# Each expert slab as two half-row transfers in place of one

## The reference

```python
def expert_choice_ffn(h, w_router, w_gate, w_up, w_down):
    cap = EC_CAPACITY * S // N_EXPERTS                 # 64 tokens for each of 16 experts
    aff = softmax(einsum('bsd,de->bse', h, w_router))
    gates, idx = lax.top_k(aff.transpose(0, 2, 1), cap)
    xe = h[bidx, idx]
    a = jnp.einsum('becd,edf->becf', xe, w_gate)       # [64 x 1024] @ [1024 x 2048], per expert
    b = jnp.einsum('becd,edf->becf', xe, w_up)         # the same shape
    ye = jnp.einsum('becf,efd->becd', jax.nn.silu(a) * b, w_down)   # [64 x 2048] @ [2048 x 1024]
    return jnp.zeros_like(h).at[bidx, idx].add(ye * gates[..., None])
```

## Time and profile before

| what | value |
|---|---|
| median of 3 runs | 2109.13 us |
| the runs | 2108.97 to 2114.0 us |
| the profiled execution | 2113.66 us |
| its span, from the first to the last instruction | 2111.9 us |
| PE busy in it | 1956.1 us, 93% |
| DMA over the whole span | 528.11 MB, mean 250 GB/s |
| mean granted clock of TensorE | 0.978 of full speed |

### The profile page before, as it was taken

The page is one execution under the profiler, slowest core; times in us unless marked ns, Lnnn a source line. Parts: engine busy times, 40 slices in busy tenths (PEclk is TensorE's granted clock), DMA queues, the critical chain, the costliest instruction groups (busy, mean ns, idle before and its releaser), DMA issues.

```text
span 2111.9 us, 23315 instructions
## 1 busy us (share of the span) xinstructions
PE 1956.1 (93%) x9049; PEld 1144.9 (54%) x9049; DVE 845.5 (40%) x1273; ACT 592.5 (28%) x917; POOL 36.7 (2%) x40
## 2 busy tenths in 40 slices
PE   7888889999999999999999988999999999999898
PEld 5656633322222222222222266888888778778786
DVE  6765431111111111111111165456456576876443
ACT  5553321110011000110010044443233343356651
POOL 1004000000000000000000000000000000000000
PEclk9988999999999999999999988999999999999999
DMA  8421579999999999999999952545345222221101
GB/s 256 140 90 35 202 292 422 422 422 422 422 422 422 422 422 422 422 422 422 422 422 422 422 183 100 198 132 186 130 160 181 80 80 81 90 70 40 41 21 40
DMA packets 132179, 528.11 MB, mean 250 GB/s; under 512 B 10006, under 2 KB 55892, under 8 KB 82836
## 3 DMA queue, kind: packets, MB, share of 16 engines
q1 hardware_dynamic: 129492, 520.56, 62.4%
q0 software_dynamic: 1008, 3.52, 0.7%
q10 hardware_dynamic: 1616, 3.15, 0.4%
HBM read 524.97 MB, written 2.23 MB: 250 GB/s over the span
## 4 chain that ended last, share of the span: by engine, by line
PE 53%; DMA 34%; DVE 6%; ACT 3%; issue 2%; SPq 1%; ACTq 0%; DVEq 0%
DMA w_expert<-in_w_up 17%; DMA w_expert<-in_w_gate 16%; PE bank L1085 6%; PE bank L868 5%; PE bank L869 5%; PE bank L870 5%; PE bank L889 5%; PE bank L891 5%; PE bank L890 5%; PE bank L908 1%; PE bank L1095 1%; DVE full L1761 1%; DMA raw<-in_w_ple_gate 1%; DVE w_lo L1698 1%; SPq L714 1%
## 5 line engine op out<-in xcount | busy, mean ns | idle before, releaser
L1085 PE MATMUL bank<-w_expert,chosen 128*64 128x512 f32 x2048 | 483.9, 602 | 63.1 <-DMA w_expert<-in_w_up 46.8
L1085 PEld LDWEIGHTS bank<-w_expert,chosen 128*64 128x64 f32 x2048 | 130.2, 136 | 396.8 <-issue 232.2
L1941 DVE TENSOR_TENSOR x_res<-x_res,bank 128x512 f32<-128x512 f32 x136 | 87.3, 683 | 428.6 <-PE bank L1104 408.2
L1095 PE MATMUL bank<-w_expert,hidden_t 128*64 128x512 f32 x1024 | 229.9, 596 | 5.9 <-ACT hidden_t L1510 4.6
L1698 DVE TENSOR_TENSOR w_lo<-raw,w_hi 128x2048 fp32r<-128x2048 f32 x75 | 173.1, 2308 | 149.2 <-ACT w_hi L1350 149.2
L1350 ACT CAST w_hi<-raw 128x2048 fp32r<-128x2048 f32 x75 | 142.9, 1905 | 158.3 <-PE bank L891 140.9
L868 PE MATMUL bank<-act_hi,w_hi 128*128 128x512 f32 x424 | 173.1, 408 | 0.1
L1963 DVE TENSOR_TENSOR hidden_rows<-gate_silu,bank 128x512 f32<-128x512 f32 x32 | 20.6, 683 | 365.2 <-PE bank L1085 365.2
L870 PE MATMUL bank<-act_hi,w_lo 128*128 128x512 f32 x424 | 166.0, 391 | 0.0
L869 PE MATMUL bank<-act_lo,w_hi 128*128 128x512 f32 x424 | 166.0, 391 | 0.0
L1095 PEld LDWEIGHTS bank<-w_expert,hidden_t 128*64 128x64 f32 x1024 | 74.6, 137 | 138.7 <-issue 121.1
(11 more groups left out here) (284 smaller groups left out, 2518.5 us busy)
## 6 DMA issues: line engine op xcount, KB each, us to landing
w_expert<-in_w_gate SPq DMA_DIRECT2D x128, 1024.0 KB, 24.9
w_expert<-in_w_up SPq DMA_DIRECT2D x128, 1024.0 KB, 26.8
w_expert<-in_w_down SPq DMA_DIRECT2D x128, 1024.0 KB, 26.6
raw<-in_a_w_in SPq DMA_DIRECT2D x24, 1024.0 KB, 6.1
raw<-in_b_w_in SPq DMA_DIRECT2D x16, 1024.0 KB, 5.3
raw<-in_a_ada_w SPq DMA_DIRECT2D x12, 1024.0 KB, 5.2
raw<-in_b_ada_w SPq DMA_DIRECT2D x12, 1024.0 KB, 6.9
raw<-in_kv_ada_w SPq DMA_DIRECT2D x8, 1024.0 KB, 5.6
```

The lines of the kernel that those rows point to most:

```text
L1085: last = mm(PS[b0 + n][HALF[x], :], XE[:, k % 4, HALF[k // 4]], WE[place][:, r], start=(k == 0), stop=(k == KD - 1), skip_group_check=True)
L1095: last = mm(PS[4][HALF[x], :], HT[:, 2 * q + k, HALF[half]], WE[place][:, r], start=(i == 0 and k == 0), stop=(i == 7 and k == 1), skip_gr ...
L1941: tt(part, part, ps[:, :], ALU.add).then_inc(d_add, 1)
```

## The change

`load_expert` issues two transfers of 512 KB in place of one of 1 MB. Each carries half of every partition's 8 KB: 1024 floats, 4 KB. For w_gate and w_up the row of 2048 floats is cut in its middle; for w_down each half is one of the two rows. Both halves raise the same semaphore by 16, so PE's wait counts in steps of 32.

```diff
@@ -711,8 +711,10 @@
                     src = (wg, wu)[i // 8][e, :, i % 8:i % 8 + 1, :]
                 else:
                     src = wd[e, down_slab(i - 16)]
-                sp.dma_start(WE[place][:, :].rearrange("p (k n) -> p k n", k=1 if i < 16 else 2), src
-                             ).then_inc(e_loaded[place], 16)
+                if i < 16:
+                    src = src.rearrange("p k (x n) -> p (k x) n", x=2)
+                for x in range(2):
+                    sp.dma_start(WE[place][:, x * D:(x + 1) * D], src[:, x, :]).then_inc(e_loaded[place], 16)
@@ -1117,7 +1119,7 @@
                     if n == 0:
                         pe.wait_ge(v_xe, e + 1)
-                    pe.wait_ge(e_loaded[place], e * (16 * SLABS_E // RING_E) + 16 * (n // RING_E + 1))
+                    pe.wait_ge(e_loaded[place], e * (32 * SLABS_E // RING_E) + 32 * (n // RING_E + 1))
```

## The result

| | before | changed |
|---|---|---|
| median | 2109.49 us | 2140.51 us |
| lowest and highest run | 2108.97 to 2114.0 | 2139.45 to 2140.76 |
| profiled execution | 2113.66 us | 2139.45 us |
| its span | 2111.9 us | 2137.7 us |

The kernel before was run once more beside the changed one, which moved its median from 2109.13 to 2109.49 us. The ratio is 1.0133, with a 95% interval of 1.0119 to 1.0146: slower by 25 to 31 us. The difference of the two medians is 31.0 us. The forecast was 2135.5 us, 26 us more than before, and the measured median lies 5.0 us above it.

What follows compares the result with a forecast made beforehand. The prediction took the DMA transfers of expert slabs as the bound: 0.072 us more for each of 365 slabs, 26.4 us, on the median 2109.13 gives 2135.5 us; SP's issues and PE's wait add nothing. Range 2115 to 2150 us.

Steps and rivals of the forecast that it cites:

- The bound: Expert stage: transfers set the pace at 2.485 us a slab; PE works 1.94 to 1.96 us, then waits about 0.55.
- The price of a slab: Expert stage: a slab in halves takes 2.557 us, 0.072 us more, for 365 slabs, 26.4 us.
- 410 GB/s row: Load of x at the start, 4 to 7 us: 512 KB transfers of 4 KB packets, taken as the halves' rate.
- second feature: Transfer size of the halves, the other feature beside packet size for choosing the load of x; 2 semaphore writes per engine.
- The two anchors: Whole kernel: adding 26.4 us gives 2140.1 us from the profiled execution, 2135.5 us from the median 2109.13.
- The cheap row: Two w_ada slabs, 1 MB transfers of 4 KB packets at 417 GB/s: 0.030 us more a slab, 11 us in all.
- cheap case: Expert stage: packet size costs 0.030 us a slab or less, semaphore writes nothing; 2120 us or less, chance 0.22.
- The dear row: w_ple_gate slabs, 2 KB packets at 386 GB/s: 9.7 ns a packet; nine more cost 0.087 us a slab, 32 us.
- The page's figure: Skill's rate for SP loads, 1 MiB per DMA and 4 KiB rows: 408.7 GB/s, 2.566 us a slab, 29 us.
- companion of that rival: Skill's setup-cost rule: about 2 us per transfer beside the bytes; prediction held it already hidden by the queue.
- that rival: SP becomes the bound in the expert stage: two issues take 3.02 us a slab, 195 us more, 2304; chance 0.03.
- The ends: Stage's start, 286 to 306 us, costs nothing more; the last down slabs' tail, 22.3 us, comes half a microsecond later.
- Theory A: Follow-up forecast: each packet has its own price, first 8.3 ns, semaphore writes included; 430 GB/s if a 16 KB row is one packet.

Runs made afterwards that it cites:

- first: Against the kernel before: still one 1 MB transfer per slab, but with 4 KB packets, the halves of a row landing swapped; 2140.07 us, ratio 1.0135.
- second experiment: Against the changed kernel: still two 512 KB transfers per slab, but with 2 KB packets; 2194.54 us, ratio 1.0394, 79 to 87 us more than the kernel before.
- fifth: Against the kernel before: only the w_down slabs go as two transfers of half a row, a third of the change; 2123.54 us, ratio 1.0047.
- sixth experiment: Against the kernel before: w_down goes as 2 MB transfers with 16 KB rows per partition; 2109.86 us against 2113.07, ratio 0.9986.
- run of streams: Separate kernel, only loads: SP streams 36 MB in each of ten forms, nothing computed; 2.486 us per MB with 8 KB packets, 2.560 with 4 KB.
- last two experiments: Against the kernel before: w_down alone in halves, ratio 1.0047; w_down alone as 2 MB transfers with 16 KB rows, ratio 0.9986.

## Why the prediction was right

**The bound.** That the transfers and not PE set the stage's pace was right, and all of the loss lies in it: 27.2 us of stage, 0.3 us behind it. But PE had less slack than the prediction's 0.55 us beside 1.94 us of matmuls suggests. Only 119 of the 365 slabs had such a wait, 62.3 us in all, which is 0.17 us per slab; the small jobs between the slabs took the rest, and PE was busy for 838.91 of 907 us. By these rows, and as an estimate, a stream faster by more than some 7% would leave the stage to PE.

**The price of a slab.** Forecast 0.072 us from the 410 GB/s row, measured 0.075 us (2.560 less 2.485) in the changed kernel. 365 x 0.075 = 27.3 us against 27.2 found. The reason that I gave for the choice of the row was half wrong: the second feature, the transfer size with its second semaphore write, costs nothing that the streams show.

**The luck in it.** That the size came out within 0.003 us a slab was luck. The earlier trace rows is a window of 3 us at the start of the kernel, and the price is a difference of 3% between two rates. The start was not changed; the same loads in the same window of the changed kernel's trace read:

```profile
DMA packets 401, 1.20 MB, mean 401 GB/s; under 512 B 74, under 2 KB 115, under 8 KB 401
```

From 401 GB/s the same working gives 2.615 us a slab, 0.130 us more, 47 us in all. In the traces of the first, second, fifth and sixth experiment this window reads 402, 401, 408 and 410. The mechanism was right with any of them, the 26 us only with the highest.

**The two anchors.** The forecast of 2135.5 us stands on the median of before, 2109.13; on the profiled execution the same sum gave 2140.1, and 2140.51 was measured. The stage and what follows account for 1.1 of the 5.0 us between forecast and measurement. The rest is where the first runs of the kernel before happened to lie: in the later comparisons its median was 2112.44 us of 7 and 2113.07 us of 17 runs.

**The cheap row.** In a steady stream 4 KB packets run at 410 GB/s, with one transfer per slab or two, so the 417 GB/s of the earlier trace rows was not their rate and the 22% on the cheap case was too much. In the run of streams, in the middle of the 4 KB form, a window of 3 us (131 to 134) and one of 4 us (124 to 128) read 415 and 410 GB/s:

```profile
DMA packets 320, 1.25 MB, mean 415 GB/s; under 512 B 16, under 2 KB 16, under 8 KB 320
...
DMA packets 419, 1.64 MB, mean 410 GB/s; under 512 B 19, under 2 KB 19, under 8 KB 419
```

Moved through that form from 102 to 162 us in steps of about half a microsecond, windows of 4 us stay within 408 to 412, those of 3 us within 407 to 415. Where a window happens to cut a slab thus does not explain 417 over 4 us. Two other readings bear on it: the 4 KB form read shortly after its start, 98 to 102 us, and the two a_ada_w slabs of the earlier trace rows in the changed kernel's trace, 44.2 to 48.2 us, which stands as long after their issue:

```profile
DMA packets 428, 1.69 MB, mean 422 GB/s; under 512 B 16, under 2 KB 16, under 8 KB 428
...
DMA packets 413, 1.63 MB, mean 407 GB/s; under 512 B 16, under 2 KB 16, under 8 KB 413
```

So a stream of 4 KB packets that has just begun reads 407, 417 and 422 in three places, and says little about a steady one. Why, stays open.

**The dear row.** 386 GB/s for 2 KB packets was right (387 in the second experiment), and the 9.7 ns that I drew from it is within 5% of the 9.3 and 9.4 ns measured. Eight packets at 9.7 ns would have given 28 us; I had added a ninth for the semaphore write.

**The page's figure.** The Trainium skill, "DMA: Bandwidth & Descriptors", the section on the iDMA fabric, with 408.7 GB/s for rows of 4 KiB, was within 0.4% of the 410 GB/s measured.

**SP.** Its issues became the largest entry of the chain and cost nothing: one and two transfers per slab give the same 410 GB/s. A fixed part of each transfer beside its bytes, the companion of that rival, does not show in the full queue: at equal packet size the rows for 256 KB and 1 MB, for 512 KB and 1 MB, and for 1 and 2 MB are equal. That the queue would take fewer slabs before it holds issues back was right: by the median from issue to landing it is 5.7 slabs in place of 10.7, which at 18 and 9 packets per slab and engine are 103 and 96 packets. But with one transfer of 4 KB packets per slab the median is 18.3 us, 7.1 slabs or 122 packets, so the packets alone do not fix it. Nothing in the sum hung on it.

**The ends.** The stretch from 286 to 306 us had room, as said: its DMA share rose from 0.88 to 0.95, its rate from 331 to 351 GB/s. Behind the last w_up slab PE came to the combine in 23.1 us (1246.22 less 1223.08) in place of 22.6, the half microsecond of the prediction. PE's waits at a slab grew to 0.62 us.

**What was outside.** Run to run the kernel before spreads over 2108.2 to 2114.8 us in the later comparisons, and the gather ahead of the stage, whose code no experiment changed, began between 272.7 and 277.5 us in the profiled executions. So a difference of two single runs says little about an effect of 3 us; the last two experiments were decided by their interval and by the length of the stage. What makes that spread stays open.

## What to carry to other kernels

Find the one resource that never pauses, here the DMA engines at a share of 1.01 while PE waits for slabs in 62 of 907 us, and price a change in its units: here packets per engine, at 9.3 ns each, times the slabs that pass it while it is saturated. Price it from a long stretch of a stream of the same shape, not from a few microseconds, where the same loads read 401 in one trace and 410 in another. In such a stage cut a load along what stays contiguous in a partition for as long as possible and do not split rows; how many transfers carry them does not matter while the queue is full.

## What the runs showed of the hardware that I had not expected

- The semaphore writes of a transfer were free in a full queue: 2.560 us per MB with one or two transfers, 2.711 and 2.710 us with one or four.
- A row of 16 KB in one partition goes as one packet and is faster than 8 KB: 429 against 422 GB/s. Theory A had this as 430 on that condition.
- Alternating transfers over partitions 0 to 63 and 64 to 127 in one queue ran at 221 to 226 GB/s with all engines busy.
